# Gate values transposed as rows behind tile 12 and normed there, and the convolution's two sums moved on TensorE

## What is computed

```
x = x + 0.5 * swiglu(rmsnorm(x, ffn1_norm), ...)
z = rmsnorm(x, mix_norm) @ w_in
q, k, v, p_in, c_in, d_in = jnp.split(z, [G, 2 * G, 3 * G, 4 * G, 6 * G], axis=-1)   # G = 256
att = moba_attention(...)
pool, pool_state = pool_mixer(pool_hist, p_in, pool_w, pool_scale)
conv, conv_state = conv_module(conv_hist, c_in, ...)   # GLU, 31 taps, layernorm over channels, silu, pointwise
gmlp, gate_v = spatial_gating(d_in, gate_norm, spatial_w, spatial_b)
x = x + jnp.concatenate([att, pool, conv, gmlp], axis=-1) @ w_out
x = x + 0.5 * swiglu(rmsnorm(x, ffn2_norm), ...)

def spatial_gating(d_in, gate_gain, spatial_w, spatial_b):
    u, v = jnp.split(jax.nn.gelu(d_in), 2, axis=-1)
    v = rmsnorm(v, gate_gain)
    ...
    s = jnp.einsum('gts,bcsgd->bctgd', w_causal, vp) + spatial_b.T[None, None, :, :, None]
    return u * s, v
```

## Time and profile before

| | |
|---|---|
| median of 3 executions | 1167.07 us (1166.45 to 1167.7) |
| the profiled execution | 1166.63 us |
| its span, first to last instruction | 1164.8 us |
| granted TensorE clock over the span | 1.0 |
| PE busy / DVE busy / ACT busy / POOL busy | 1155.5 / 742.6 / 540.7 / 114.7 us |

### The profile page before, as it was taken

How to read it: one execution, slowest core, us unless ns; L and a number is a source line. 1 busy time by engine, 2 the same in 40 slices (tenths; PEclk the granted TensorE clock), 3 DMA queues, 4 the chain that set the end, 5 groups by cost and what they waited for, 6 DMA issues and landing times.

```text
span 1164.8 us, 22491 instructions
## 1 busy us (share of the span) xinstructions
PE 1155.5 (99%) x7942; PEld 1137.6 (98%) x7942; DVE 742.6 (64%) x1239; ACT 540.7 (46%) x825; POOL 114.7 (10%) x164
## 2 busy tenths in 40 slices
PE   8999999999999999999999999999999999999999
PEld 8999999999899999999999999999987999999998
DVE  7767665579667666655566676655896676665442
ACT  6444444445855444444454444444468554443332
POOL 0000000037810000000000000000577000000000
PEclk9999999999999999999999999999999999999999
DMA  7644435557435444435564444455572454444453
GB/s 242 208 152 153 144 100 161 149 175 224 138 129 176 146 154 150 136 113 150 170 207 147 155 149 135 116 147 172 185 242 75 149 176 146 156 148 123 136 149 106
DMA packets 71789, 180.24 MB, mean 155 GB/s; under 512 B 10122, under 2 KB 25282, under 8 KB 71746
## 3 DMA queue, kind: packets, MB, share of 16 engines
q1 hardware_dynamic: 71026, 178.36, 49.2%
q10 hardware_dynamic: 720, 1.34, 0.3%
HBM read 176.09 MB, written 3.58 MB: 154 GB/s over the span
## 4 chain that ended last, share of the span: by engine, by line
PE 95%; DVE 2%; ACT 1%; DMA 1%; issue 0%; ACTq 0%; DVEq 0%
PE bank L573 31%; PE bank L574 30%; PE bank L576 30%; ACT prob L1038 0%; DMA x<-in_xT 0%; DVE prob L1395 0%; DVE bank L1259 0%; PE bank L824 0%; DMA raw<-in_w 0%; PE bank L796 0%; PE bank L588 0%; PE bank L753 0%; ACT L1041 0%; PE bank L817 0%; PE bank L793 0%
## 5 line engine op out<-in xcount | busy, mean ns | idle before, releaser
L896 ACT ACTIVATE w_hi<-raw 128x1024 fp32r<-128x1024 f32 (+2 forms) x351 | 337.2, 961 | 470.7 <-PE bank L576 456.5
L573 PE MATMUL bank<-xg_hi,w_hi 128*128 128x320 f32 x1632 | 507.4, 311 | 1.3 <-DVE w_lo L1126 1.3
L576 PE MATMUL bank<-xg_hi,w_lo 128*128 128x320 f32 x1632 | 504.3, 309 | 0.0
L574 PE MATMUL bank<-xg_lo,w_hi 128*128 128x320 f32 x1632 | 504.3, 309 | 0.0
L1126 DVE TENSOR_TENSOR w_lo<-raw,w_hi 128x1024 fp32r<-128x1024 f32 (+2 forms) x319 | 347.7, 1090 | 153.8 <-ACT w_hi L896 149.1
L573 PEld LDWEIGHTS bank<-xg_hi,w_hi 128*128 128x128 f32 x1632 | 306.3, 188 | 4.9 <-issue 3.3
L574 PEld LDWEIGHTS bank<-xg_lo,w_hi 128*128 128x128 f32 x1632 | 306.3, 188 | 0.7
L576 PEld LDWEIGHTS bank<-xg_hi,w_lo 128*128 128x128 f32 x1632 | 306.3, 188 | 0.0
L573 PE MATMUL bank<-h_hi,w_hi 128*128 128x320 f32 x704 | 217.5, 309 | 0.0
L574 PE MATMUL bank<-h_lo,w_hi 128*128 128x320 f32 x704 | 217.5, 309 | 0.0
L576 PE MATMUL bank<-h_hi,w_lo 128*128 128x320 f32 x704 | 217.5, 309 | 0.0
(11 more groups left out here) (208 smaller groups left out, 739.0 us busy)
## 6 DMA issues: line engine op xcount, KB each, us to landing
raw<-in_w SPq DMA_DIRECT2D x223, 512.0 KB, 3.8
raw<-in_w SPq DMA_DIRECT2D x64, 384.0 KB, 3.1
raw<-in_w SPq DMA_DIRECT2D x64, 320.0 KB, 2.9
k_all<-in_cache_kT SPq DMA_DIRECT2D x32, 128.0 KB, 2.9
v_past<-in_cache_v SPq DMA_DIRECT2D x32, 128.0 KB, 3.1
x<-in_xT ACTq DMA_DIRECT2D x4, 320.0 KB, 5.4
out_yT<-x SPq DMA_DIRECT2D x1, 960.0 KB, 4.8
out_kT<-qk SPq DMA_DIRECT2D x2, 320.0 KB, 4.4
```

What stands on the lines that cost most here:

```text
L573: pe.matmul(out, hi, in_hi[:, k, :], start=first and m == 0, stop=False)
L574: pe.matmul(out, hi, in_lo[:, k, :], start=False, stop=False)
L576: mm = pe.matmul(out, lo, in_hi[:, k, :], start=False, stop=last and end)
L896: act.activation(w_hi[:, j, 0:count * P], raw[:, j, 0:count * P], ACT.Copy).then_inc(split_hi.sem, 1)
```

## The change

In PE's order the gate values' transposes move up behind tile 12, where the sums of squares stood, and work on values that are neither normed nor multiplied by the gain. DVE copies them from PSUM to SBUF (`w_tok`, `w_tok_s`); ACT squares the rows with a running sum (the norm is now a sum along the free axis), takes the roots, and scales the rows in place. The gain and the bias are put in by DVE behind the spatial matmuls. The bias matmuls, the small spreading matmul and DVE's masking go; the block-diagonal spatial weights of the sample tokens come by eight DMAs, the bias by four. The convolution's mean moves from behind tile 13 to behind tile 14, its variance from ahead of tile 15 to behind `prompt_attention`. Two sequences' pages are loaded ahead of the weights of tile 8.

```diff
@@ load_small
-                for lane in (0, 32):
-                    sp.dma_start(b_sp[lane:lane + HEADS, :], sp_b[L, :, :]).then_inc(small_in.sem, 16)
+                for g in range(HEADS):
+                    sp.dma_start(b_sp[64 * (g % 2):64 * (g % 2) + 64, g // 2, :], sp_b[L, g, :].partition_broadcast(64)).then_inc(small_in.sem, 16)
+                for b in range(DEC_B):
+                    sp.dma_start(w_sps[b * DEC_T:(b + 1) * DEC_T, :, b, :], sp_wT[L, 0:DEC_T, :, 0:DEC_T]).then_inc(small_in.sem, 16)
@@ SP, tiles 8 to 15
-                for n in range(DEC_B // 4):
+                for b in range(2):
+                    load_past(L, b)
+                for n in range(2):
...
-                        load_past(L, n * 4 + j)
+                        if 2 + n * 4 + j < DEC_B:
+                            load_past(L, 2 + n * 4 + j)
@@ value_rows
-                pe.wait_ge(sp_ok.sem, sp_ok.at(L, 5))
-                pe.matmul(bank[0][0:NS, 256:288].rearrange("p (g t) -> p g t", g=HEADS), views["e8"][0:8, :],
-                          w_sp[0:8, :, 0:DEC_T], start=True, stop=True).then_inc(sp_rep.sem, 1)
@@ PE
-            def gate_square_sum(L):
...
+            def gate_value_rows(L):
+                pe.wait_ge(gelu_ok.sem, gelu_ok.at(L, 2))
                 pe.wait_ge(p_biased.sem, p_biased.at(L, 8))
...
+                for c in range(GT):
+                    for t in range(2):
+                        pe.transpose(bank[6][:, t * 2 * P + c * P:t * 2 * P + (c + 1) * P], z_w[:, c, t * P:(t + 1) * P], ident)
+                for c in range(GT):
+                    mm = pe.transpose(gate_rows[c], z_w[:, c, SEQ:TOK], ident)
+                mm.then_inc(gm_tr.sem, 1)
@@ prompt_attention_transposes
-                pe.wait_ge(gm_rt.sem, gm_rt.at(L, 2))
+                pe.wait_ge(gm_raw.sem, gm_raw.at(L, 3))
@@ spatial_gates
-                for c in range(GT):
-                    pe.matmul(bank[2 + c][:, 0:TOK], gsel[:, c, :], bias_sp[:, :], start=True, stop=False, skip_group_check=True)
@@ batch_probabilities
-                pe.wait_ge(gm_copied.sem, gm_copied.at(L, 3))
+                pe.wait_ge(cv_rt.sem, cv_rt.at(L, 1))
@@ PE's order
                 batch_scores(L)
-                gate_square_sum(L)
+                gate_value_rows(L)
                 column(L, BASE_I, T_I, 1, 3, 1)
+                column(L, BASE_I, T_I, 1, 3, 2)
                 conv_mean(L)
-                column(L, BASE_I, T_I, 1, 3, 2)
                 prompt_attention_transposes(L)
                 value_rows(L)
+                column(L, BASE_I, T_I, 1, 3, 3)
+                prompt_attention(L)
                 conv_variance(L)
-                column(L, BASE_I, T_I, 1, 3, 3)
-                gate_value_rows(L)
-                prompt_attention(L)
                 batch_probabilities(L)
                 spatial_gates(L)
@@ ACT
-                gate_value(1)
+                gelu(z_w[:, 1, :], T_I + 11)
...
+                for c in range(GT):
+                    act.wait_ge(cv_cent.sem, cv_cent.at(L, c + 1))
+                    act.activation(conv_sq[:, c, :], conv_y[:, c, :], ACT.Square).then_inc(cv_sq.sem, 1)
+                act.wait_ge(gm_raw.sem, gm_raw.at(L, 3))
+                for n, rows in enumerate((w_tok[:, 0, :], w_tok[:, 1, :], w_tok_s[:, :])):
+                    act.activation(gm_junk[n][0:rows.shape[0], :], rows, ACT.Square, accum_out=gm_sums[n]).then_inc(gm_sum.sem, 1)
                 round_slot(L, BASE_O, 0, 0, HALVES8)
                 act.preload_act_table(ACT.Sqrt)
-                act.wait_ge(gm_sum.sem, gm_sum.at(L, 1))
...
-                for c in range(GT):
-                    act.wait_ge(cv_cent.sem, cv_cent.at(L, c + 1))
-                    act.activation(conv_sq[:, c, :], conv_y[:, c, :], ACT.Square).then_inc(cv_sq.sem, 1)
+                act.wait_ge(gm_sum.sem, gm_sum.at(L, 3))
+                for out, total in gm_root:
+                    act.activation(out, total, ACT.Sqrt, bias=eps_rms[0:out.shape[0], :], scale=1.0 / (GT * P)).then_inc(gm_rt.sem, 1)
                 round_slot(L, BASE_O, 0, 1, HALVES8)
...
                 act.activation(conv_root[:, :], bank[7][:, 0:TOK], ACT.Sqrt, bias=eps_ln, scale=1.0 / (GT * P)).then_inc(cv_rt.sem, 1)
-                act.wait_ge(gm_tr.sem, gm_tr.at(L, 1))
                 act.wait_ge(gm_inv.sem, gm_inv.at(L, 2))
                 for t in range(2):
...
+                    act.activation(w_tok[:, t, :], w_tok[:, t, :], ACT.Identity, scale=gm_scale[0][:, t:t + 1]).then_inc(gm_copied.sem, 1)
@@ DVE
-                dve.wait_ge(gm_sq_ok.sem, gm_sq_ok.at(L, 2))
-                dve.tensor_tensor(gm_sq[:, 0, :], gm_sq[:, 0, :], gm_sq[:, 1, :], ALU.add).then_inc(gm_added.sem, 1)
...
+                dve.wait_ge(gm_tr.sem, gm_tr.at(L, 1))
...
+                dve.tensor_copy(w_tok[:, :, :].rearrange("p t n -> p (t n)"), bank[6][:, :]).then_inc(gm_raw.sem, 1)
+                for c in range(GT):
+                    dve.tensor_copy(w_tok_s[:, c * P:(c + 1) * P], gate_rows[c]).then_inc(gm_raw.sem, 1)
...
-                dve.tensor_tensor(w_sps[:, :, :, :],
...
+                dve.wait_ge(gm_rt.sem, gm_rt.at(L, 2))
+                for n in range(2):
+                    dve.reciprocal(gm_scale[n], gm_root[n][0]).then_inc(gm_inv.sem, 1)
+                dve.wait_ge(v_copied.sem, v_copied.at(L, 1))
                 dve.wait_ge(cv_rt.sem, cv_rt.at(L, 1))
                 dve.reciprocal(conv_inv, conv_root[:, :]).then_inc(cv_ln.sem, 1)
...
+                    dve.scalar_tensor_tensor(out=prompt, in0=prompt, scalar=gain_g, in1=b_sp[:, c:c + 1, :].to_broadcast([P, 2, P]),
+                                             op0=ALU.mult, op1=ALU.add).then_inc(gm_biased.sem, 1)
+                    dve.scalar_tensor_tensor(out=rows, in0=rows, scalar=gain_g, in1=b_sp[:, c:c + 1, 0:DEC_T].to_broadcast([P, DEC_B, DEC_T]),
+                                             op0=ALU.mult, op1=ALU.add).then_inc(gm_biased.sem, 1)
```

More of the change, by code:

```diff
@@ L209, in hybrid_decoder @@
         qk_root = tmp[:, 2, :]
-        gm_sq = tmp[:, 0:2, :]
-        gm_root = (stat[:, 40:42], stat[0:NS, 42:43])
-        gm_scale = (stat[:, 43:45], stat[0:NS, 45:46])
+        gm_sums = (stat[:, 40:41], stat[:, 41:42], stat[0:NS, 42:43])
+        gm_root = ((stat[:, 43:45], stat[:, 40:42]), (stat[0:NS, 45:46], stat[0:NS, 42:43]))
+        gm_scale = (stat[:, 46:48], stat[0:NS, 48:49])
         gated = tmp[:, 4:6, :]
+        gm_junk = [tmp[:, n, 0:GT * P] for n in (2, 3, 5)]
         conv_sq = tmp[:, 0:2, :]
@@ L336, in hybrid_decoder @@
         conv_inv = bank[1][:, 0:TOK]
+        gate_rows = [bank[4 + c][0:NS, KEYS:KEYS + P] for c in range(GT)]
         conv_sum = bank[7][:, :].rearrange("p (c t) -> p c t", c=GT)
@@ L757, in spatial_gates @@
             def spatial_gates(L):
-                pe.wait_ge(sp_ok.sem, sp_ok.at(L, 6))
+                pe.wait_ge(sp_ok.sem, sp_ok.at(L, 2))
                 pe.wait_ge(gm_copied.sem, gm_copied.at(L, 3))
                 pe.wait_ge(taken.sem, taken.at(L, T_O))
-                for c in range(GT):
-                    pe.matmul(bank[2 + c][:, 0:TOK], gsel[:, c, :], bias_sp[:, :], start=True, stop=False, skip_group_check=True)
                 for c in range(GT):
@@ L767, in spatial_gates @@
                             pe.matmul(bank[2 + c][lanes, t * P:(t + 1) * P], w_tok[:, t, g * 64:(g + 1) * 64], w_sp[:, g, :],
-                                      start=False, stop=False, skip_group_check=True)
+                                      start=True, stop=True)
                 for c in range(GT):
@@ L1011, in _ @@
                 round_slot(L, BASE_I, 3, 1, HALVES8)
-                gate_value(0)
+                gelu(z_w[:, 0, :], T_I + 9)
                 round_slot(L, BASE_I, 3, 2, HALVES8)
@@ L1039, in _ @@
                                        scale=stat[:, 24 + 4 * t + h:25 + 4 * t + h]).then_inc(p_norm.sem, 1)
-                round_slot(L, BASE_O, 0, 0, HALVES8)
-                act.preload_act_table(ACT.Sqrt)
-                act.wait_ge(gm_sum.sem, gm_sum.at(L, 1))
-                act.activation(gm_root[0], bank[6][:, 0:2], ACT.Sqrt, bias=eps_rms, scale=1.0 / (GT * P)).then_inc(gm_rt.sem, 1)
-                act.activation(gm_root[1], bank[6][0:NS, 2:3], ACT.Sqrt, bias=eps_rms[0:NS, :], scale=1.0 / (GT * P)).then_inc(gm_rt.sem, 1)
                 for c in range(GT):
@@ L1099, in _ @@
                 act.wait_ge(gate_tr.sem, gate_tr.at(L, 1))
-                act.activation(gate_s[:, :, :].rearrange("p c t -> p (c t)"), bank[4][:, TOK:TOK + GT * NS], ACT.Copy).then_inc(rows_ok.sem, 1)
+                for c in range(GT):
+                    last = act.activation(gate_s[:, c, :], bank[4][:, TOK + c * NS:TOK + (c + 1) * NS], ACT.Identity,
+                                          scale=vec[:, bass.ds(L * NV + (V_GG + c), 1)])
+                last.then_inc(rows_ok.sem, 1)
                 for i in range(IT_O):
@@ L1428, in _ @@
```

(3 more changed lines are left out.)

80 lines of the change are left out of this document (21 added, 59 removed).

## The result

The changed kernel takes 1183.32 us (median of 4 runs, 1182.02 to 1184.97) against 1166.97 us before: a ratio of 1.0137, interval 1.0125 to 1.0148. I had forecast 1173.4 us, at most 1176.4. The direction was right; the loss is 16.35 us and not 6.4. The profiled execution is the longest of the four, 1184.97 us around a span of 1183.2 us, so differences of the two traces are summed to its own 18.34 us.

A forecast was written before the change was run, and what follows sets the result against it. PE's list was taken as the bound (busy 99%). 0.45 + 2.77 and 0.39 + 2.77 us give 6.38 us, taking 1166.63 to 1173.0 us; with 0.44 us for the median, 1173.4 us, range 1171.4 to 1176.4 us.

The forecast's parts named there:

- What bounds the kernel: PE is busy 99% of the span, so a change wins only from PE's list or its few waits.
- What leaves PE's list: Per layer: sums of squares even with transposes, 0.49 us bias, at most 0.30 us spreading, roots' wait; first layer's 0.50 us gap.
- the page loads: Pages ahead of tile 8's weights: remove the first layer's 0.50 us gap before sample scores; 2 x 3.37 us at worst, hidden.
- The first wait: PE waits over 2 us for ACT ahead of the attention, which starts 0.45 us late in layer 1, 0.39 in layer 2.
- the longer sum of 1176.2 us: Total if ACT's table switch also costs the Trainium skill's drain, 1.38 us more per layer on top of 1.28 us.
- The second wait: From the attention to the first spatial product: variance, root, reciprocal and tile 15 uncovered, 5.79 us against 3.02, adding 2.77 a layer.
- What I cost at nothing: Raw-row copies, gain and bias, row scaling, tile 15's gelu, small DMAs and page loads, all taken as hidden under other work.
- The raw copies: DVE's three copies of raw rows ahead of the sum for the mean: 1.2 us, hidden by the mean's later place.
- The gain-and-bias steps: Four DVE instructions between spatial products and gating product: at most 1.8 us, ends 0 and 0.9 us a layer, taken as 0.
- The sum: 0.45 + 2.77 and 0.39 + 2.77 us over the two layers: 6.38 us slower.
- rival 1: TensorE's clock falls in the gaps ahead of attention and spatial products: 1175.8 us once a layer, 1178.2 twice; chance 0.13.
- the ten steps: Ten steps behind the gap at the kernel's start took 2.67 us against 0.151 us a step: 1.2 us lost per clock fall.

The follow-up runs named there:

- both back: Changed kernel with the convolution's mean back behind tile 13 and its variance back ahead of tile 15: 1166.36 us, ratio 0.9992 to the kernel before.
- the first gap alone filled: Changed kernel with 12 unused matmuls of ones by ones ahead of the attention only, later gaps left empty: 1181.83 us, ratio 1.0123.
- three steps moved: Mean and variance back in the changed kernel, plus raw-row copies behind the sum, tile 15 taken ahead of the reciprocal, output slots 1 and 2 rounded later: 1164.88 us.
- all gaps filled: Changed kernel with 12, 2 and 7 unused matmuls ahead of attention, sample probabilities and spatial products: 1174.29 us, ratio 1.0059.
- only 0.7 us empty: Changed kernel with 12 and 7 unused matmuls ahead of attention and spatial products, none ahead of the sample probabilities: 1174.37 us, ratio 1.0059.
- the 1.9 us gap alone: Changed kernel with 12 and 2 unused matmuls ahead of attention and sample probabilities, none ahead of the spatial products: 1179.3 us, ratio 1.0104.

## Why the prediction was wrong

- **What bounds the kernel**, PE's list, was read right, and the loss lies where the prediction looked.
- **What leaves PE's list.** The transposes for the sums of squares: 0.63 us (298.66 to 299.29) for 0.74 us, even as said. The gap ahead of the sample scores is gone, but the reason I gave, the page loads, is not supported: with the old order of loads it did not come back either.
- **The first wait** was right in its sum. I had 7.24 + 9.34 = 16.58 us from tile 13 to the attention; it is 16.37 us in both layers. The three squares with a running sum take 1.20 us and not 1.47, as ACT's rows of the changed kernel show below: the first of them and the rounding behind the last, with the 1.92 us in which ACT stands for DVE's subtraction. Behind the table load ACT goes on at once (load at 310.71 for 1.28 us, next activation at 312.00), so nothing here supports the longer sum of 1176.2 us.

```profile
307.68 0.87 ACT L1016 ACTIVATE tmp<-conv_y 128x320 f32<-128x320 f32 x2 [1.92 <-DVE conv_y L1400]
308.45 0.40 ACT L1019 ACTIVATE tmp<-w_tok 128x256 f32<-128x256 f32 x1
...
309.65 1.04 ACT L877 ACTIVATE w_hi<-raw 128x1024 fp32r<-128x1024 f32 x1
```

- **The second wait** was right: 5.79 us predicted from the attention to the spatial products, 6.00 us in layer 1. The order on DVE is as I read it, root, reciprocal, and tile 15 queued behind:

```profile
318.83 2.16 DVE L1423 RECIPROCAL bank<-tmp 128x320 f32<-128x320 f32 x1 [6.10 <-ACT tmp L1036]
321.03 0.49 DVE L1222 TENSOR_TENSOR z_u<-bank,rms 128x320 f32<-128x320 f32 x1
```

- **What I cost at nothing.** The raw copies hid behind the later mean, as said. Where that cover is taken away (both back) PE waits 1.3 and 0.9 us ahead of the mean; with the copies moved behind the sum as well, 0.8 of these 2.3 us remain, so the copies cost some 1.5 us in both layers together. The gain-and-bias steps cost nothing visible in the changed kernel. The page loads had a second reader that I missed: pages pass the weight slots, ACT's rounding waits for a slot, and queued behind it on ACT are the squares that the query and key sums need. ACT's rows of the changed kernel:

```profile
277.05 1.06 ACT L877 ACTIVATE w_hi<-raw 128x1024 fp32r<-128x1024 f32 x1 [3.20 <-DMA raw<-in_w]
278.02 0.45 ACT L968 ACTIVATE tmp<-qk 128x320 f32<-128x320 f32 x1
```

PE waited 0.37 us there, and up to 1.0 us in other runs, but under 0.2 us in some with the same loads (the one with the first gap alone filled, and the one with three steps moved). I had looked only at the use of the slot itself, three columns later.

- **The sum.** 6.38 us; with the clock kept up by fillers the kernel is 7.2 us over before (1174.29 less 1167.11). That step was short by under 1 us.
- **The failed step is the fall of TensorE's clock (rival 1)**: the forecast's sum puts it at nothing, and the rival priced it too low and with it got too small a chance. I priced a fall at 1.2 us from the ten steps behind the gap at the kernel's start, and gave it 0.13, because gaps of 0.5 and 0.63 us in the mixers of before had left the clock at 1.0. A fall here costs 4.41 us in layer 1 and 1.48 and 4.20 us in layer 2, as the clock then stays at 0.50, for 9 us of unbroken work in layer 1. The ten steps were no measure of that, and I misread them: PE had been as slow ahead of that gap. Both rows here are the same matmuls of ones by ones, the first at the start of the kernel before, 0.23 us a step (4.64 us for 20), the second as fillers in the run with all gaps filled, 0.12 us a step (2.84 us for 24):

```profile
1.16 4.64 PE L618 MATMUL bank<-ones 128*128 128x128 f32 x20 [1.16 <-DVE ones L1115]
...
311.26 2.84 PE L812 MATMUL bank<-ones 128*128 128x128 f32 x24
```

So the ten steps were the end of a slow start and not a fall behind a gap. The windows view has the granted clock at 1.00 all through that start and says nothing of the slow steps. The run with only 0.7 us empty agrees with the rows of 0.5 and 0.63 us (1174.37 us); but they said nothing of gaps of 2 us and more, and such I had worked out myself. At 4.3 us, the mean of the two long ones, one fall a layer on top of my 1173.4 us gives 1182.0 us; 1183.32 us was measured. The Trainium skill's sentence that I set beside it (TensorE: Matmul & The Clock Gate, "Part 1: The HAM clock gate"), by which throttled is the default state and activity releases it, agrees with the trace of the changed kernel in its first half: 0.50 behind the idle gaps, from 322 us on. For the second half the trace shows a release only at 331 us, behind 9 us of unbroken work.

## What to carry to other kernels

When a change opens a gap of microseconds on a TensorE that was never idle, price the clock as well as the gap: here 9 us of the 16 came from work at half clock behind it. Whether that is the cause takes one run, with filler matmuls in the gap: if more work makes the kernel faster and the granted clock stays up, it was the clock. And a step that others wait for should not move behind the work that covered its chain: follow the chain over every engine's in-order list (mean, subtraction, squares, table, copies) before moving its first link.

## What was not expected of the hardware

- The granted clock stayed at 0.50 for some 10 us (321 to 331 us, and 905 to 915 us) although PE was busy in all of the windows between from 322 and 906 on.
- A gap of 1.9 us cost no less (5.0 us) than one of 3.1 us (3.6 us; the runs overlap), and one and the same gap of 3.1 us dropped the clock in one layer and not in the other of a single execution. What decides beyond the gap's length stays open.
- With the 1.9 us gap alone the clock fell only after PE had worked again for more than 1.6 us (1.00 at 320 to 322, 0.57 at 322 to 324), so the slow stretch need not begin where the gap is.
